# First value unit ahead of the query units and FFN2's first unit with tokens stationary, both tile by tile, in a one-core transformer kernel

## The reference

```
x    = x + 0.5 * swiglu(rmsnorm(x, g1), ffn1_w_in, ffn1_w_out)        # FFN1: 1024 -> 2 x 2816 -> 1024
xn   = rmsnorm(x, mix_g)
proj = xn @ w_mix_in            # q, k, v, o (1024 each), i and f gates (4 each), z (2048), gate_m, gate_s
h_m  = sigmoid(o) * layernorm(mlstm(silu(conv(q,k)), v, i, f)) * head_g
h_s  = u * (w_s @ layernorm(v2)),  u, v2 = gelu(z)
x    = x + (sigmoid(gate_m) * h_m + sigmoid(gate_s) * h_s) @ w_mix_out
x    = x + 0.5 * swiglu(rmsnorm(x, g2), ffn2_w_in, ffn2_w_out)        # FFN2
out  = rmsnorm(x, final_g)
swiglu(x, w_in, w_out): gate, up = split(x @ w_in);  (silu(gate) * up) @ w_out
```

## Time and profile before

| | us |
|---|---|
| median of 3 runs | 1273.7 |
| lowest, highest | 1269.09, 1273.74 |
| profiled execution: its time | 1273.71 |
| profiled execution: span from first to last instruction | 1272.0 |
| FFN1 in the trace | about 649 to 837 |
| mix stage | about 842 to 1073 |
| FFN2 | about 1078 to 1266 |

### The profile page before, as it was taken

One profiled execution on the slowest core, in us unless ns is written; L12 is line 12 of the kernel. 1 busy time (PEld: TensorE's weight loads), 2 busy tenths in 40 slices (PEclk: granted clock), 3 DMA queues, 4 the chain that ended last, 5 costly groups with the idle time before them and its releaser, 6 DMA issues.

```text
span 1272.0 us, 16338 instructions
## 1 busy us (share of the span) xinstructions
PE 1069.6 (84%) x7178; PEld 809.3 (64%) x7178; DVE 515.2 (41%) x609; ACT 402.7 (32%) x482; POOL 39.8 (3%) x69
## 2 busy tenths in 40 slices
PE   6999999565656473748789999999999999999998
PEld 4995594222222131313379998899888778999986
DVE  3544542211102020202175454358644886555543
ACT  2435632000000000000064434356535535444432
POOL 1001200000000000000000000000000220000000
PEclk9999899877878786969999999999999999999999
DMA  9897889999999999999976545545454354665530
GB/s 365 302 367 277 327 304 376 427 428 429 427 428 428 428 428 428 428 424 421 396 247 208 171 175 198 176 180 199 137 195 158 115 190 150 201 196 199 183 116 33
DMA packets 111778, 358.17 MB, mean 282 GB/s; under 512 B 8388, under 2 KB 56152, under 8 KB 97368
## 3 DMA queue, kind: packets, MB, share of 16 engines
q1 hardware_dynamic: 110072, 353.63, 72.2%
q10 hardware_dynamic: 1632, 3.45, 0.9%
HBM read 356.01 MB, written 1.05 MB: 281 GB/s over the span
## 4 chain that ended last, share of the span: by engine, by line
PE 69%; DMA 23%; DVE 5%; SPq 1%; ACT 1%; issue 1%; POOL 0%; DVEq 0%; ACTq 0%
PE psum L1975 17%; PE psum L1977 17%; PE psum L1976 17%; DMA spare<-in_moe_w_down_dram 7%; DMA ring<-in_moe_w_down_dram 5%; DMA spare<-in_moe_w_gate_dram 5%; PE psum L2261 4%; PE psum L2295 3%; DMA spare<-in_moe_w_up_dram 2%; DMA ring<-in_moe_w_up_dram 2%; DMA ring<-in_ada_w_dram 2%; PE psum L2248 2%; PE psum L2208 1%; PE psum L2303 1%; PE psum L2025 1%
## 5 line engine op out<-in xcount | busy, mean ns | idle before, releaser
L1588 DVE TENSOR_TENSOR wl<-ring,wh 128x2048 fp32r<-128x2048 f32 x101 | 231.8, 2302 | 231.5 <-ACT wh L1080 231.5
L1080 ACT ACTIVATE wh<-ring 128x2048 fp32r<-128x2048 f32 x102 | 195.1, 1916 | 307.8 <-PE psum L1977 290.2
L1975 PE MATMUL psum<-hTh,wh 128*128 128x256 f32 x832 | 235.3, 283 | 0.2 <-DVE wl L1588 0.2
L1976 PE MATMUL psum<-hTl,wh 128*128 128x256 f32 x832 | 234.9, 282 | 0.0
L1977 PE MATMUL psum<-hTh,wl 128*128 128x256 f32 x832 | 234.7, 282 | 0.0
L1975 PEld LDWEIGHTS psum<-hTh,wh 128*128 128x128 f32 x832 | 158.7, 191 | 0.6 <-DVE wl L1588 0.4
L1977 PEld LDWEIGHTS psum<-hTh,wl 128*128 128x128 f32 x832 | 158.7, 191 | 0.0
L1976 PEld LDWEIGHTS psum<-hTl,wh 128*128 128x128 f32 x832 | 158.6, 191 | 0.0
L2261 PE MATMUL psum<-ring,m_xT 128*32 128x512 f32 x448 | 97.7, 664 | 66.4 <-DMA spare<-in_moe_w_up_dram 50.2
L2261 PEld LDWEIGHTS psum<-ring,m_xT 128*32 128x32 f32 x448 | 26.0, 121 | 119.8 <-issue 115.2
L1547 DVE TENSOR_TENSOR m_h<-m_sg,psum 128x512 f32<-128x512 f32 x8 | 8.2, 1027 | 213.7 <-PE psum L2261 175.1
(11 more groups left out here) (347 smaller groups left out, 1599.9 us busy)
## 6 DMA issues: line engine op xcount, KB each, us to landing
ring<-in_ffn_w_in_dram SPq DMA_DIRECT2D x44, 1024.0 KB, 7.7
ring<-in_moe_w_down_dram SPq DMA_DIRECT2D x16, 2048.0 KB, 32.9
ring<-in_w_mix_in_dram SPq DMA_DIRECT2D x32, 1024.0 KB, 6.9
ring<-in_moe_w_gate_dram SPq DMA_DIRECT2D x15, 2048.0 KB, 29.3
ring<-in_moe_w_up_dram SPq DMA_DIRECT2D x13, 2048.0 KB, 30.2
ring<-in_ada_w_dram SPq DMA_DIRECT2D x24, 1024.0 KB, 13.2
spare<-in_moe_w_up_dram SPq DMA_DIRECT2D x11, 2048.0 KB, 30.7
ring<-in_ffn_w_out_dram SPq DMA_DIRECT2D x20, 1024.0 KB, 6.2
```

The lines of the kernel that those rows point to most:

```text
L1080: a.activation(dst, src, ACT.Copy).then_inc(split_h, 1)
L1588: v.tensor_tensor(split_half(h, wl), raw_half(h), split_half(h, wh).bitcast(FP32), ALU.subtract)\
L1975: t.matmul(dst, sh, mh, start=first, stop=False, skip_group_check=True)
L1976: t.matmul(dst, sh, ml, start=False, stop=False, skip_group_check=True)
```

## The change

1. Of the mix units the first value unit, `("v", 0)`, is moved to the front, ahead of "if" and q. It runs tile by tile (`tile_first`), and `turn(3, 1, *)` stand between its products. `turn(3, 0, *)` go into the last pass of FFN1's tail, after its 6th and 9th matmul of 12; the tail has two pairs now instead of three.
2. FFN2's first in-unit has tokens stationary and 256 weight columns (gate and up) moving, tile by tile (`unit_by_tokens`); `turn(5, 1, *)` stand between its products. Its silu and product are made by token tile, and TensorE transposes the product back (`transposed_product`, four transposes between the halves of unit 1).
3. A fourth split buffer (`wh_extra`, `wl_extra`) holds the second half of these two units. Both halves of the v unit are split at the end of FFN1's down stage, and both halves of FFN2's first unit ahead of the norm.
4. The fillers at both boundaries go. ScalarE and VectorE take the work of the first v unit with the q units; the later split calls move up by one unit.

```diff
         for j in range(FF // 256):
-            plan.use(("gate", n, j), bank=2 * (j % 2))
-            plan.use(("up", n, j), bank=2 * (j % 2) + 1)
+            if n and not j:
+                for tt in range(NT):
+                    plan.use(("tok", tt), bank=tt)
+                plan.use(("actT",), bank=4)
+            else:
+                plan.use(("gate", n, j), bank=2 * (j % 2))
+                plan.use(("up", n, j), bank=2 * (j % 2) + 1)
...
     transposes(3)
+    for tt in range(NT):
+        plan.use(("mv", 0, tt))
...
             plan.use(("ws",))
-    for u in range(2):
-        for tt in range(NT):
-            plan.use(("mv", u, tt))
+    for tt in range(NT):
+        plan.use(("mv", 1, tt))
...
         wl = [area(f"wl{i}", spl_at[i][1], HALF, dt=F32R) for i in range(SPLITS)]
+        wh.append(area("wh_extra", REST, HALF, dt=F32R))
+        wl.append(area("wl_extra", REST + HALF, HALF, dt=F32R))
...
                     "gm": 6 * D + 2 * MH, "gs": 7 * D + 2 * MH}
-        mix_units = [("q", 0), ("q", 1), ("k", 0), ("k", 1), ("v", 0), ("v", 1), ("z", 2), ("z", 3),
+        mix_units = [("v", 0), ("q", 0), ("q", 1), ("k", 0), ("k", 1), ("v", 1), ("z", 2), ("z", 3),
...
+        extra_halves = [first_half[at_b["mix", "v", 0]] + 1, first_half[at_b["in", 1, 0]] + 1]
+        extra_after = first_half[at_b["down", 0, 3]] + 1
+        assert 2 * HALF <= 16 * T
+        in_turn = [h for h in range(len(halves)) if h not in extra_halves]
+        split_turn = {h: i for i, h in enumerate(in_turn)}
...
+        def split_buffer(h):
...
+            return split_turn[h] % SPLITS if h in split_turn else SPLITS
...
+        def await_buffer(eng, h):
...
+            if h == extra_halves[0]:
+                await_half_used(eng, extra_after)
+            elif h == extra_halves[1]:
+                for half in range(2):
+                    await_copied(eng, ("sv", 1, half))
+            elif split_turn[h] >= SPLITS:
+                await_half_used(eng, in_turn[split_turn[h] - SPLITS])
...
                         act.wait_ge(wb_in[n % RING_B], 32 * (n // RING_B + 1))
-                    if h >= SPLITS:
-                        await_half_used(act, h - SPLITS)
+                    await_buffer(act, h)
...
                 def silu(j):
+                    if n and not j:
+                        for tt in range(NT):
+                            b = await_full(act, ("tok", tt))
+                            a.activation(by_gate(sil, tt), by_gate(b)[:, :, 0, :], ACT.Silu).then_inc(tok_s, 1)
+                        return
...
                 def high(j):
+                    if n and not j:
+                        b = await_full(act, ("actT",))
+                        a.activation(actTh[:, 0:2, :], by_k(b, 2), ACT.Copy).then_inc(act_h, 1)
+                        return
...
                     step(base + n_in + j)
-                split_to(first_half[base + n_in + n_out - 1] + 1)
+                split_to(first_half[base + n_in + n_out - 1] + (1 if n else 3))
...
                 high_of_hT(3, 0, half)
-            split_to(first_half[mix0] + 1)
...
+            def v_copy(u):
+                b = await_full(act, ("mv", u, 0))
+                emptied(a.activation(vx[:, 0, 2 * u:2 * u + 2, 0:MD], by_k(b, 2), ACT.Copy), ("mv", u, 0))
...
-            step(mix0, forget)
+            step(mix0)
+            step(mix0 + 1, lambda: v_copy(0), forget)
...
-                split_to(first_half[mix0 + u + 2] + 1)
+                split_to(first_half[mix0 + u + 3] + 1)
...
                 tap(2 * u + 1)
-                split_to(first_half[mix0 + u + 2] + 2)
+                split_to(first_half[mix0 + u + 3] + 2)
...
             step(mix0 + 16)
-            split_to(first_half[mix0 + 18] + 1)
+            split_to(first_half[mix0 + 18] + 2)
...
                 def product(j):
+                    if n and not j:
+                        for tt in range(NT):
+                            b = await_full(dve, ("tok", tt))
+                            dve.wait_ge(tok_s, tt + 1)
+                            emptied(v.tensor_tensor(by_gate(prod, tt), by_gate(sil, tt), by_gate(b)[:, :, 1, :],
+                                                    ALU.mult), ("tok", tt))
+                        for tt in range(NT):
+                            await_copied(dve, ("tok", tt))
+                        dve.sem_inc(prod_s, 1)
+                        return
...
                     dve.wait_ge(act_h, n * n_in + j + 1)
+                    if n and not j:
+                        emptied(v.tensor_tensor(actTl[:, 0:2, :], by_k(bank(("actT",)), 2),
+                                                actTh[:, 0:2, :].bitcast(FP32), ALU.subtract), ("actT",))
+                        await_copied(dve, ("actT",))
+                        dve.sem_inc(rest_s, 1)
+                        return
...
                     step(base + n_in + j)
-                split_to(first_half[base + n_in + n_out - 1] + 1)
+                split_to(first_half[base + n_in + n_out - 1] + (1 if n else 3))
...
             uT = small[0:MH, 168:168 + T]
-            mix0 = at_b["mix", "q", 0]
+            mix0 = at_b["mix", "v", 0]
...
             step(mix0 + 16, lambda: mixed(0, 0), lambda: mixed(0, 1))
-            split_to(first_half[mix0 + 18] + 1)
+            split_to(first_half[mix0 + 18] + 2)
...
+            def unit_by_tokens():
...
+                banks = [open_bank(pe, ("tok", tt)) for tt in range(NT)]
+                taken_halves = []
+                for tt in range(NT):
+                    for f in range(2):
+                        if tt == 0:
+                            taken_halves.append(next_half())
+                        h, uh, ul, _ = taken_halves[f]
+                        for k in range(KD):
+                            if f == 0 and k % 4 == 0:
+                                await_copied(pe, ("T", 5, tt, k // 4))
+                            if (tt, f) == (0, 1) and k in (4, 6):
+                                turn(5, 1, k // 2 - 2)
+                            tok = slice(P * tt, P * tt + P)
+                            last = product(banks[tt][:, T * f:T * f + T], (hTh[:, k, tok], hTl[:, k, tok]),
+                                           (uh[:, k].rearrange("p w n -> p (w n)"),
+                                            ul[:, k].rearrange("p w n -> p (w n)")), k == 0, k == KD - 1)
+                        if f == 1:
+                            filled(last, ("tok", tt))
+                        elif tt == 1:
+                            half_done(h, last)
...
+            def transposed_product():
...
+                pe.wait_ge(prod_s, n_in + 1)
+                b = open_bank(pe, ("actT",))
+                for f in range(2):
+                    for tt in range(NT):
+                        last = t.transpose(b[:, T * f + P * tt:T * f + P * tt + P], by_gate(prod, tt)[:, f, :], ident)
+                filled(last, ("actT",))
...
                 for j in range(n_in):
+                    if n and not j:
+                        unit_by_tokens()
+                        continue
...
                     for f in range(2):
+                        if n and j == f == 1:
+                            transposed_product()
...
                                 if j == f == i == 0 and k % 4 == 0:
-                                    await_hT(5 if n else 2, k // 4)
+                                    await_hT(2, k // 4)
...
-                for pair in range(NF // 2 - 3):
+                tail = 3 if n else 2
+                for pair in range(NF // 2 - tail):
...
                 for tt, halves_of_row in ((0, (0, 1)), (1, (0,)), (1, (1,))):
-                    for i in range(3):
-                        pair = NF // 2 - 3 + i
+                    for i in range(tail):
+                        pair = NF // 2 - tail + i
...
                                 last = down(c, tt, half, weights)
+                            if n == 0 and halves_of_row == (1,) and (i, c % 2) in ((0, 1), (1, 0)):
+                                turn(3, 0, i)
...
                             half_done(h, last)
-                    if n == 0 and halves_of_row == (0,):
-                        for half in range(2):
-                            turn(3, 0, half)
...
             keep_busy(open_bank(pe, ("gate", 0, 0)), 1)
+            def turns_of_second_tile(i, tt, k):
...
+                if i == tt == 0 and k == 0:
+                    await_copied(pe, ("T", 3, 0, 0))
+                if i == 1 and tt == 0:
+                    if k == 0:
+                        await_copied(pe, ("T", 3, 0, 1))
+                    elif k >= 2:
+                        turn(3, 1, k - 2)
+                if tt == 1 and k == 0:
+                    await_copied(pe, ("T", 3, 1, i))
...
             ffn(0)
-            for half in range(2):
-                turn(3, 1, half, 1 if half else 10)
-            keep_busy(open_bank(pe, ("if",)), 4)
```

(36 more changed lines are left out.)

## The result

| | before | changed |
|---|---|---|
| median, 17 runs each | 1270.37 us | 1263.43 us |
| lowest to highest | 1268.5 to 1276.07 | 1262.73 to 1269.41 |
| profiled execution, span | 1272.0 | 1263.7 |

The ratio of the runs is 0.9949, 95% interval 0.9938 to 0.996: 5 to 8 us less, 6.5 at the middle, so faster by about the half per cent that can be told from no change. The forecast was 5.3 us less, and 1268.4 us with a range of 1265.0 to 1272.5. The time measured lies 1.6 us under the range.

A forecast was written before the change was run, and what follows sets the result against it. TensorE was taken as the bound, with time to win only where it stands, does unused work or runs slowly. Winning 2.2 us at FFN1 to mix and 3.1 at mix to FFN2, 5.3 together, gave 1268.4 us, range 1265 to 1272.5.

The forecast's parts named there:

- The start of the sum: Whole kernel: the profiled execution, 1273.71 us with span 1272.0, taken as equal to the median of the runs.
- wait and cut turn at `turn(3, 0, *)`: FFN1's tail: TensorE waits 0.74 us at the first turn, and cutting the turn in two costs 0.11 more.
- wait ahead of v: FFN1 to mix: TensorE waits 1.20 us before the first v product, until tile 0's `hTl` frees its bank.
- the turn: Both boundaries: 0.11 us per transpose and 0.11 for the return, so four transposes by themselves cost 0.55 us.
- VectorE's lateness behind the splits: End of FFN1: VectorE begins tile 0's down sum at 831.92, 1.36 us late, because two splits stand in front.
- ScalarE's square in front of `hTh`: First boundary: tile 1's square precedes tile 0's `hTh` in ScalarE's queue, so `hTl` begins at 838.5.
- the two late turns at the second boundary: Mix output: a third rest part delays the norm 1.08 us; TensorE waits 0.2 and 0.3 at `turn(5, 0, *)`.
- the three places without a wait: No TensorE wait before `turn(3, 1, *)`, before `turn(5, 1, *)` or before the transposes of the product.
- the gaps close fully: Rival, both boundaries: waits of 0.74, 1.20 and 0.50 us absent, 7.7 us won, 1266.0 us; chance 0.20.
- the clock falls at the boundaries: Rival: half clock costs 1.6 us at one boundary, 3.2 at both, giving 1270.0 to 1271.6 us; chance 0.15.
- The transposed product: Rival, FFN2: product late, TensorE waits 5.6 us between unit 1's halves, 1274.0 us; chance 0.06.
- Order within mix: Rival, mix: waits move to the first score or a q half, 2 to 4 us, 1270.5 to 1272.5; chance 0.07.

The follow-up runs named there:

- `before_again`: The kernel before, same program, run once more for its trace; single time 1270.51 us.
- `v_first_only`: The kernel before with only the first boundary changed (value unit first, tail of two pairs), FFN2 as before; median 1267.99 us, ratio to before 0.9976.
- `ffn2_only`: The kernel before with only the second boundary changed (FFN2's first unit by token tiles, product transposed), q first in mix; median 1267.29 us, ratio to before 0.9969.
- `high_first`: The changed kernel with ScalarE's two copies of tile 0's hTh put ahead of the square of tile 1's first half; median 1263.93 us, ratio to before 0.9937.
- `early_splits`: The changed kernel with extra-buffer halves split before their sisters and the last mix unit's second half before the mix sums; median 1262.68 us, ratio to before 0.9926.
- `before_no_filler`: The kernel before without its filler matmuls at the two boundaries, waits and order as before; median 1274.16 us, ratio 1.0031.
- `after_again`: The changed kernel, same program, run once more for its trace; single time 1269.09 us.

## Why the prediction was wrong, point by point

**The start of the sum was the step that failed.** The prediction took the profiled execution (1273.71) as typical because it "equals the median of the runs", three of them. Seventeen runs put the median at 1270.37, 3.3 us lower. `before_again`, whose run (1270.51) is near that median, shows where it lies, in two equal parts: the profiled run had the fall of the clock behind line 2423 and the second had not, 1.6 us; and the first split of FFN1 stands at 652.12 in the one and at 650.50 in the other, 1.6 us ahead of the whole block. What brings this second part is open. The prediction named this fall (rows 7), and put its absence only at the low end of the range, for the changed kernel; it belonged in the start, since it is chance in both kernels. (The two together, 7.7 and 1.6 off 1273.7, make 1264.4 and not the 1265 stated; the time measured is under that too.) From 1270.37 the same sum gives 1265.1, and the range 1261.7 to 1269.2.

**The difference was somewhat small**, 5.3 us against 6.1 in the traces and 6.5 (5 to 8) by the ratio. Boundary by boundary:

| term | predicted | measured in the changed kernel |
|---|---|---|
| first: wait and cut turn at `turn(3, 0, *)`, beyond the old 0.87 of both | 0.85 | 0.67 |
| first: wait ahead of v, net of the short return | 1.20 | 1.31 |
| first: `turn(3, 1, *)` | 1.10 | 0.88 |
| first boundary, won | 2.2 | 2.5 by these terms, 2.8 in `v_first_only` |
| second: waits at `turn(5, 0, *)` | 0.50 | 0.48 |
| second: `turn(5, 1, *)` | 1.10 | 0.88 |
| second: unit 1's first half | 0.10 | 0.17 |
| second: transposes of the product | 0.55 | 0.43 |
| second boundary, won | 3.1 | 3.4 by these terms, 3.5 in `ffn2_only` |

The mis-sized term is the turn. I read 0.99 us for eight transposes from the first load after them, and charged 0.11 for the return on top for each group of four. But the load behind the return comes 0.11 after it instead of 0.234, which gives the return back: eight cost 0.87 and four 0.44. The trace of before had it, one row behind those of the earlier trace rows; without the turn the second load would stand at 832.13 + 0.234 = 832.36:

```profile
833.12 0.19 PEld L1975 LDWEIGHTS psum<-wh,actTh 128*128 128x128 f32 x1
833.23 0.19 PEld L1976 LDWEIGHTS psum<-wl,actTh 128*128 128x128 f32 x1
```

Six groups by 0.11 make 0.66 of the 0.8 us.

**The mechanism was right.** VectorE's lateness behind the splits (831.36 in the changed trace, 831.92 - 0.61 = 831.31 predicted, as the changed trace runs 0.61 ahead at the start of the block), ScalarE's square in front of `hTh`, the two late turns at the second boundary and the three places without a wait came where the prediction put them. `high_first` and `early_splits` took the causes away one by one, and the waits went with them.

**The rivals.** That the gaps close fully didn't come true; the waits are there. That the clock falls at the boundaries didn't either: 1.00 in both traces of the changed kernel there. `before_no_filler` shows that the worry was justified for the old order, at a bare wait of 2.94 us; in the changed order, with waits of 0.9 and 1.5 us, it didn't come. The transposed product was ready 0.8 us early. Order within mix: from the decay matmuls to the last mix splits nothing was lost (the distance shrank by 11.3 us for a unit of 11.2 that left).

So of the 5.0 us between the forecast and the median 3.3 are the start and 0.8 the difference in the block, 5.3 against 6.1, of which the terms of the table place 0.6. The last 0.8 lie between the traces' 6.1 and the 6.9 of the medians (the ratio gives 6.5); they aren't placed, and they are inside the interval.

## What to carry to other kernels

When a stage boundary leaves the matmul engine waiting for a norm, look for a unit of the next stage that can be done by token tile, and let the first tile's products cover the second tile's norm; fillers then have nothing to do. Look at once at what the new early work pushes back on the helper engines: here two splits moved ahead of a sum, and a square ahead of a copy, gave 3 of 9 us back, and both were mended by the order of the calls. And don't take the one profiled run for the median: compare stretches between two fixed points in several traces before a total is forecast.

## What the runs showed of the hardware

- The granted clock behind the decay matmuls was at half level in seven of the first ten traces and at 1.00 in three, of the same and of changed programs. The two pairs of traces of one program price it at 1.6 us. It accounts for a part of the 7 us between runs of one kernel. More lies ahead of FFN1, where no run's edit reaches: the first split stands between 649.00 (`ffn2_only`) and 653.58 (`after_again`). No run here shows why.
- A bare wait of 2.94 us with eight transposes behind it was followed by half clock at both boundaries, at a cost of 1.0 and 2.3 us; waits of 0.9 and 1.5 us within 4.4 us, with transposes between them, were not.
- Four transposes between products cost 0.44 us, and after a wait only 0.27 beyond the wait itself (from 834.33, where TensorE arrived, to 835.17 the wait of 0.84; the whole displacement was 1.10).
- Products with 128 tokens stationary and 256 weight columns moving ran at the rate of the other form: 0.12 us each.
